# The chunk-wise inverse of the odd layer in 32x32 blocks, with two products per round side by side

## The reference, cut to what matters

```python
kk = jnp.einsum('bhntd,bhnsd->bhnts', kc, kc)
m = jnp.where(strict, betac[..., :, None] * kk * gam, 0.0)
rhs = jnp.concatenate([vc * betac[..., None], kc * (betac * jnp.exp(bc))[..., None]], axis=-1)
sol = lax.linalg.triangular_solve(m + jnp.eye(CHUNK, dtype=F32), rhs, left_side=True,
                                  lower=True, unit_diagonal=True)
u, w = sol[..., :C_DV], sol[..., C_DV:]
...
def step(state, xs):                      # over the 4 chunks
    v_new = u_i - w_i @ state
    o = qd_i @ state + qk_i @ v_new
    state = gl_i * state + kd_i.T @ v_new
```

## Time and profile before

| | us |
|---|---|
| median of 3 runs | 586.52 |
| profiled execution, device time | 586.91 |
| its span, first to last instruction | 584.7 |
| TensorE busy | 541.3 |
| VectorE busy | 328.9 |
| ScalarE busy | 254.0 |
| GpSimd busy | 81.4 |

### The profile page before, as it was taken

How to read it: one execution, slowest core, us unless ns; L and a number is a source line. 1 busy time by engine, 2 the same in 40 slices (tenths; PEclk the granted TensorE clock), 3 DMA queues, 4 the chain that set the end, 5 groups by cost and what they waited for, 6 DMA issues and landing times.

```text
span 584.7 us, 12159 instructions
## 1 busy us (share of the span) xinstructions
PE 541.3 (93%) x5162; PEld 445.5 (76%) x5162; DVE 328.9 (56%) x595; ACT 254.0 (43%) x501; POOL 81.4 (14%) x98
## 2 busy tenths in 40 slices
PE   6999799999899999789999999999999889999975
PEld 6999799996565645359989998999889656664632
DVE  3579876657334333377996555467445633334335
ACT  5576467664233323155546434433226323331311
POOL 5716621100000000021003900011110000000000
PEclk9999999998999999999999799999789989999999
DMA  9991333787899999997463430000315979989992
GB/s 319 272 371 58 108 109 110 228 305 295 312 408 409 375 411 409 390 376 243 160 215 80 176 109 2 4 4 2 145 34 225 411 282 411 408 347 412 407 409 109
DMA packets 55671, 144.16 MB, mean 247 GB/s; under 512 B 4292, under 2 KB 29088, under 8 KB 55488
## 3 DMA queue, kind: packets, MB, share of 16 engines
q1 hardware_dynamic: 54496, 141.88, 64.6%
q0 software_dynamic: 944, 1.41, 1.2%
q10 hardware_dynamic: 176, 0.07, 0.1%
HBM read 142.30 MB, written 1.05 MB: 245 GB/s over the span
## 4 chain that ended last, share of the span: by engine, by line
PE 75%; DVE 14%; ACT 5%; issue 3%; POOL 1%; DMA 1%; ACTq 0%; DVEq 0%
PE PS L2097 11%; PE PS L2058 7%; PE PS L2119 6%; PE PS L610 6%; PE PS L611 5%; PE PS L612 5%; PE PS L2133 4%; PE PS L646 3%; DVE WL L606 3%; PE PS L648 2%; PE PS L647 2%; PE PS L2134 2%; PE PS L2467 2%; PE PS L2488 2%; DVE SL L1303 2%
## 5 line engine op out<-in xcount | busy, mean ns | idle before, releaser
L606 DVE TENSOR_TENSOR WL<-RAW,WH 128x768 fp32r<-128x768 f32 (+2 forms) x90 | 82.0, 947 | 30.2 <-ACT WH L592 29.8
L610 PE MATMUL PS<-WH,HTH 128*128 128x384 f32 (+2 forms) x272 | 93.2, 343 | 3.0 <-DVE HTL L1295 1.4
L611 PE MATMUL PS<-WL,HTH 128*128 128x384 f32 (+2 forms) x272 | 90.1, 331 | 0.0
L612 PE MATMUL PS<-WH,HTL 128*128 128x384 f32 (+2 forms) x272 | 90.0, 331 | 0.0
L1295 DVE TENSOR_TENSOR X<-PS,X 128x512 f32<-128x512 f32 (+2 forms) x84 | 53.9, 663 | 48.0 <-PE PS L2134 36.1
L592 ACT ACTIVATE WH<-RAW 128x768 fp32r<-128x768 f32 (+2 forms) x90 | 67.2, 793 | 4.8 <-PE PS L612 3.1
L610 PEld LDWEIGHTS PS<-WH,HTH 128*128 128x128 f32 x272 | 53.5, 197 | 4.4 <-DVE HTL L1295 1.7
L611 PEld LDWEIGHTS PS<-WL,HTH 128*128 128x128 f32 x272 | 53.7, 197 | 0.0
L992 ACT ACTIVATE SIL<-PS,MW 128x128 f32<-128x128 f32 x18 | 6.6, 367 | 107.6 <-PE PS L2097 98.0
L612 PEld LDWEIGHTS PS<-WH,HTL 128*128 128x128 f32 x272 | 53.3, 196 | 0.0
L646 PE MATMUL PS<-HTH,WH 128*128 128x256 f32 x160 | 46.0, 287 | 0.4 <-DVE HTL L1303 0.4
(11 more groups left out here) (362 smaller groups left out, 1060.8 us busy)
## 6 DMA issues: line engine op xcount, KB each, us to landing
RAW<-moe_w_down SPq DMA_DIRECT2D x32, 512.0 KB, 13.1
RAW<-moe_w_gate SPq DMA_DIRECT2D x32, 512.0 KB, 7.8
RAW<-moe_w_up SPq DMA_DIRECT2D x32, 512.0 KB, 8.6
XD<-moe_w_down SPq DMA_DIRECT2D x32, 512.0 KB, 13.4
XG<-moe_w_gate SPq DMA_DIRECT2D x32, 512.0 KB, 9.2
XG<-moe_w_up SPq DMA_DIRECT2D x32, 512.0 KB, 10.3
RAW<-od_w_in SPq DMA_DIRECT2D x9, 1536.0 KB, 7.8
RAW<-ev_w_in SPq DMA_DIRECT2D x5, 1536.0 KB, 15.4
```

The costliest lines, as they stand in the source:

```text
L606: done(nc.vector.tensor_tensor(out=lo, in0=raw, in1=hi.bitcast(F32), op=ALU.subtract), "unit_lo")
L610: nc.tensor.matmul(ps, ah, bh, start=start, stop=False)
L611: nc.tensor.matmul(ps, ah, bl, start=False, stop=False)
L612: return nc.tensor.matmul(ps, al, bh, start=False, stop=stop)
```

## The change

The inverse inside a chunk is now built from 32x32 blocks for levels 0 to 4. The array is used as four 32x32 tiles on its diagonal (`quarters`), one per block of 32 frames. A round has two steps on TensorE instead of three. `inverse_TQ` issues the transpose of YC and the product of NTD with the half of YC's columns that this level uses (16 of 32 columns) into one bank; ScalarE copies both with one instruction of 384 columns (before: two of 512). `inverse_Z` multiplies the two (16 columns), and VectorE writes the result with two masked copies of 128 elements (before: one of 512). Level 0's entries come from a product with the identity (`inverse_N`) and the same masked copies, not from NTD directly. Level 5 joins 32x32 blocks in the same two steps with 64-wide pieces. Level 6 keeps 64x64 products, but its transpose is no longer waited for by its first product, and everything goes to `UT`, a full 128x128 block per head and tile whose zero quarter GpSimd clears. Each solve is then one 128x128 by 64 product per head instead of two. Group 1 stands one level behind group 0 in all engines' programs. The mask table grows by three 128-column layers, and on VectorE some elementwise steps of mixer D and of the gates stand later.

```diff
             def inverse_X(g, L):
-                rows = slice(0, P if L < 6 else CH)
                 act.wait_ge(sem(f"c_T{g}"), L)
-                done(nc.scalar.activation(heads(XC, g)[rows], level_ps(0, g)[rows], ACT.Copy), f"c_X{g}")
-
-            def inverse_Q(g, L):
-                rows = slice(0 if L < 6 else CH, P)
-                act.wait_ge(sem(f"c_Q{g}"), L)
-                done(nc.scalar.activation(heads(QC, g)[rows], level_ps(2, g)[rows], ACT.Copy), f"c_Qs{g}")
+                done(nc.scalar.activation(XC[:, g, :], PS[:, g, 0:384], ACT.Copy), f"c_X{g}")
+
+            def inverse_last_Q(g):
+                act.wait_ge(sem(f"c_Q{g}"), 1)
+                done(nc.scalar.activation(QC[CH:P, g, :, :], PS[CH:P, 2 + 2 * g, :].rearrange("p (n t) -> p n t", n=8), ACT.Copy),
+                     f"c_Qs{g}")
+            def inverse_upper(g, c):
+                act.wait_ge(sem(f"c_T{g}"), 6)
+                rows = slice(CH * c, CH * c + CH)
+                done(nc.scalar.activation(UT[rows, 0::2, 4 * g:4 * g + 4, rows],
+                                          PS[rows, g, :].rearrange("p (h i t) -> p i h t", h=4, i=2), ACT.Copy), f"c_Qs{g}")
...
+            inverse_X(0, 4)
+            inverse_X(1, 3)
+            inverse_X(0, 5)
+            inverse_X(1, 4)
+            inverse_last_Q(0)
+            inverse_upper(0, 1)
+            inverse_X(1, 5)
+            inverse_upper(0, 0)
+            inverse_last_Q(1)
+            inverse_upper(1, 1)
+            solved(0, 0, 1)
+            inverse_upper(1, 0)
+            solved(0, 1, 2)
-            solved(0, 0, 1)
-            solved(0, 1, 2)
...
+            def placed(g, L, b):
+
+                c = 2 ** (L + 1)
+                for half in range(2):
+                    cols = slice(32 * half, 32 * half + 32)
+                    to = YC[:, 4 * g:4 * g + 4, :, cols].rearrange("p h i (m c) -> p (h i) m c", c=c)[:, :, :, 0:c // 2]
+                    m1 = MKC[:, L, cols].rearrange("p (m c) -> p m c", c=c)[:, :, 0:c // 2]
+                    z = PS[:, b, 0:128].rearrange("p (n m c) -> p n m c", n=8, c=c // 2)
+                    done(nc.vector.copy_predicated(to, m1.unsqueeze(1).to_broadcast([P, 8, 32 // c, c // 2]), z), f"c_Y{g}")
...
+                if L < 5:
+                    placed(g, L, 2 + 2 * g)
...
                 else:
-                    done(nc.vector.tensor_copy(YS[0:CH, :, hs, :], z[0:CH]), f"c_Y{g}")
+                    z = PS[0:CH, 3 + 2 * g, :].rearrange("p (h i t) -> p i h t", h=4, i=2)
+                    done(nc.vector.tensor_copy(UT[0:CH, 0::2, hs, CH:P], z), "c_ys")
...
+            query_scores(2)
             dve.wait_ge(sem("dg_in"), 32)
             link(tt(xc2, xc2, bc(DG[:, :], 1, [P, 2, 512]), MUL))
-            inverse_level(0, 4)
-            inverse_level(1, 4)
-            query_scores(1)
+            inverse_level(1, 6)
+            query_scores(3)
             link(tt(xc2, xc2, bc(DB[:, :], 1, [P, 2, 512]), ADD))
+            residue(0, 1)
             dve.wait_ge(sem("gate_t"), 2)
             link(stt(tg, tg, 1.0, TM[:, :, 1552:2064], ADD, MUL))
-            inverse_level(0, 5)
-            inverse_level(1, 5)
             done(stt(TM[:, :, 1552:2064], xc2, 0.5, tg, MUL, MUL), "d_mix")
-            query_scores(2)
+            residue(1, 2)
+            out_split(1, 0)
+            lhs_lo(3, D_PIECES)
             dve.wait_ge(sem("gate_t"), 1)
             link(stt(SG[:, :, :], SG[:, :, :], 1.0, TM[:, :, 0:512], ADD, MUL))
-            inverse_level(0, 6)
-            inverse_level(1, 6)
-            query_scores(3)
             link(stt(g16, g16, 0.5, bc(CGAIN, 1, [P, 16, 64]), MUL, MUL))
-            out_split(1, 0)
-            lhs_lo(3, D_PIECES)
-            residue(0, 1)
             out_split(1, 1)
-            residue(1, 2)
             norm_sum(0, 0, 1)
             norm_sum(1, 0, 2)
...
-                return [(i, h) for i in range(NT) for h in range(4 * g, 4 * g + 4)]
+                return [(i, h) for h in range(4 * g, 4 * g + 4) for i in range(NT)]
...
+            def inverse_N(g):
+                pe.wait_ge(sem("c_nt"), 2 * g + 1)
+                for n, (i, h) in enumerate(group(g)):
+                    for q, rows in enumerate(quarters):
+                        last = mm(PS[rows, g, 16 * n:16 * n + 16], key_block(q, i, h), first_half(ident[rows, rows], 0),
+                                  start=True, stop=True)
+                done(last, f"c_N{g}")
...
+            def inverse_TQ(g, L):
+                pe.wait_ge(sem(f"c_Y{g}"), 2 * L)
+                if L < 5:
+                    for n, (i, h) in enumerate(group(g)):
+                        for q, rows in enumerate(quarters):
+                            mm(PS[rows, g, 32 * n:32 * n + 32], inverse_block(q, i, h), ident[rows, rows], start=True, stop=True)
+                    for n, (i, h) in enumerate(group(g)):
+                        o = 256 + 16 * n
+                        for q, rows in enumerate(quarters):
+                            last = mm(PS[rows, g, o:o + 16], key_block(q, i, h), first_half(inverse_block(q, i, h), L),
+                                      start=True, stop=True)
...
+                    for i, h in group(g):
+                        o = CH * (h % 4)
+                        for c, rows in enumerate(halves):
+                            mm(PS[strip(c, i), g, o:o + CH], YC[rows, h, i, 32:64], ident[rows, rows], start=True, stop=True)
+                    for i, h in group(g):
+                        o = 256 + 32 * (h % 4)
+                        for c, rows in enumerate(halves):
+                            b = 256 * i + CH * c + 32
+                            last = mm(PS[strip(c, i), g, o:o + 32], NTD[rows, h, b:b + 32], YC[rows, h, i, 0:32], start=True, stop=True)
                 done(last, f"c_T{g}")
...
+                for n, (i, h) in enumerate(group(g)):
+                    if L < 5:
+                        for q, rows in enumerate(quarters):
+                            last = mm(PS[rows, 2 + 2 * g, 16 * n:16 * n + 16], XC[rows, g, 32 * n:32 * n + 32],
+                                      XC[rows, g, 256 + 16 * n:256 + 16 * n + 16], start=True, stop=True)
...
+            def inverse_last(g):
+                pe.wait_ge(sem(f"c_Y{g}"), 12)
+                for n, (i, h) in enumerate(group(g)):
+                    last = mm(PS[high, 2 + 2 * g, CH * n:CH * n + CH], NTD[low, h, 256 * i + CH:256 * i + P], YC[low, h, i, :],
+                              start=True, stop=True)
                 done(last, f"c_Q{g}")
+                for n, (i, h) in enumerate(group(g)):
+                    for rows in halves:
+                        last = mm(PS[rows, g, CH * n:CH * n + CH], YC[rows, h, i, :], ident[rows, rows], start=True, stop=True)
+                done(last, f"c_T{g}")
+
+            def inverse_last_Z(g):
+                pe.wait_ge(sem(f"c_Qs{g}"), 2)
+                for n, (i, h) in enumerate(group(g)):
+                    last = mm(PS[low, 3 + 2 * g, CH * n:CH * n + CH], QC[high, g, n, :], UT[high, 2 * i, h, CH:P], start=True, stop=True)
                 done(last, f"c_Z{g}")
...
                 for h in range(4 * g, 4 * g + 4):
                     hs = slice(256 * i + (h % 4) * 64, 256 * i + (h % 4) * 64 + 64)
-                    mm(PS[low, 2 * i + g, hs], YC[low, i, h, :], rhs[low, h, :], start=True, stop=True)
-                    last = mm(PS[high, 2 * i + g, hs], YS[:, i, h, :], rhs[:, h, :], start=True, stop=True)
+                    last = mm(PS[:, 2 * i + g, hs], UT[:, 2 * i, h, :], rhs[:, h, :], start=True, stop=True)
                 done(last, "c_U")
...
             pe.wait_ge(sem("proj_ev"), proj_total[1])
+            inverse_N(0)
             key_scores(1)
+            inverse_TQ(0, 1)
             retention_scores(1)
-            pe.wait_ge(sem("c_nt"), 3)
-            for L in range(1, 7):
-                inverse_T(0, L)
-                inverse_T(1, L)
+            pe.wait_ge(sem("c_nt"), 2)
+            inverse_Z(0, 1)
+            inverse_N(1)
+            inverse_TQ(0, 2)
+            inverse_TQ(1, 1)
+            retention_out()
+            inverse_Z(0, 2)
+            inverse_Z(1, 1)
+            inverse_TQ(0, 3)
+            inverse_TQ(1, 2)
+            inverse_Z(0, 3)
+            inverse_Z(1, 2)
+            values_T()
+            inverse_TQ(0, 4)
+            inverse_TQ(1, 3)
+            inverse_Z(0, 4)
+            inverse_Z(1, 3)
+            query_scores(0)
+            inverse_TQ(0, 5)
+            inverse_TQ(1, 4)
+            inverse_Z(0, 5)
+            inverse_Z(1, 4)
+            query_scores(1)
+            inverse_last(0)
+            inverse_TQ(1, 5)
+            inverse_last_Z(0)
+            inverse_Z(1, 5)
+            query_scores(2)
+            inverse_last(1)
             first_rows(0)
+            query_scores(3)
+            inverse_last_Z(1)
+            residue(0, 1)
             first_rows(1)
```

(62 more changed lines are left out.)

96 lines of the change are left out of this document (39 added, 57 removed).

## The result

| | before | changed |
|---|---|---|
| median of runs (5 of each), us | 586.25 | 604.99 |
| lowest to highest, us | 584.36 to 588.19 | 601.68 to 612.72 |
| profiled span, us | 584.7 | 603.2 |
| first record of the output projection, us | 420.31 | 440.27 |
| from there to the end of the span, us | 164.4 | 162.9 |

The ratio is 1.0321, with a 95% interval of 1.0275 to 1.0367. The forecast was 576.1, range 571 to 588: wrong in its sign, and outside its range. The last two lines of the table say where to look: all of the loss lies ahead of the first output unit, where I had forecast 9 us of gain.

The account below looks back on a forecast made before the run. TensorE's pace was taken as the bound. 15.9 us of its work removed, less 5.5 of added waits, gave 10.4 off the profiled 586.9, so 576.5, and a median of 576.1; range 571 to 588.

Parts of the forecast that it names:

- TensorE's pace: Inverse levels: four 32x32 blocks side by side take 8.3 ns a record, so 1,664 records take 13.8 us.
- My own sign for it: In a T step, 64 records would start over 0.5 us, not 0.9 or more.
- The burst of 10 ns: Layer 0 before the change: four records in different blocks start within 0.03 us, at most 10 ns apart.
- the 20 ns over 48 records: Layer 0 before the change: fastest sustained pace seen, four positions used, a third of the records with 128 columns moving.
- Rival A: TensorE cannot issue faster than seen sustained: 594.5 at 20 ns a record, 611.4 at 29.2; chance 0.12 and 0.03.
- Waits laid bare: TensorE's idle in the inverse and its tail grows from 2.7 to 8.2 us, 5.5 more.
- The three waits of the tail: After `inverse_last_Z(1)`, TensorE waits 0.8 us for the residue, 0.75 for `d_mix` and 3.0 before `outputs(1, 0)`.
- Masked copies: VectorE's 128-element copies in the inverse levels take 0.35 us each, two 0.7, as much as the one before.
- The solves: Four solves after the inverse go from 8.2 us to 3.4, at 8 records per call and 104 ns each.
- The clock: One fall to half clock expected again in the new tail, as before, costing 3.3 us: no gain and no loss.
- Rival B: Half clock in the 32-wide stretch, levels 1 to 4: some 15 us more, 591; chance 0.05.
- a sign of being wrong: Records over 12 ns apart, VectorE taking over the chain, or the clock at 0.5 before the solves.

Follow-up runs that it names:

- the streams: Kernel before with two streams of unused independent products, 32x32 then 64x64, 2,048 records each, put ahead of the first solve; the streams took 56 and 58 us.

## Why the prediction was wrong

**The step that failed is TensorE's pace.** I took 8.3 ns a record "because rows 3 and 4 show the block's own time and not the issue deciding", over 1,664 records. The block's time was right (8.6 ns measured). My own sign for it, 64 records of a T step starting over 0.5 us, came true (0.55) while the kernel lost. A record also needs two instructions, and I never asked whether these can be had at that rate; the term has no line for them. The burst of 10 ns in the earlier trace rows is shorter than a piece of 256 instructions, so it could not show this; the 20 ns over 48 records are no limit either, for the same reason. The price that counts is 27.5 to 28.5 ns a record when it goes on (29.1 over the twelve pieces of the changed kernel), and the steps of the kernel before, at 29.2 ns, stood only 2 to 6% above the streams' price. The query scores between them give some room: with them a round is 200 records in 6.61 us, 33 ns each.

**The sum with the right term.** 1,664 records are 3,328 instructions, 13 pieces, and at 3.5 us each 46 us. I had 13.8 for their array time, 32 less. The first output unit was forecast about 9 us before 420.31, near 411, and came at 440.27, 29 later. So this one term accounts for the miss in its size.

**Rival A was the right one**, with 0.15 of the chance. Its first price (20 ns, 594.5) was too low, its second (29.2 ns, 611.4) 6 us too high. It added the price of the small records to that of the wide products beside them, but pieces keep coming under those: from 376.77 to 387.96 three pieces came, 3.73 us each, though 24 of their records are retention products that alone hold TensorE for 5.2 us. The argument against it was the burst. The Trainium skill ("TensorE: Matmul & The Clock Gate", "Wait — 56ns, not 53.3ns?") led to an estimate near 604 by another reason, a start-to-start floor near 25 ns. The time fits, the reason does not: within a piece records started 8.6 ns apart. The Trainium skill ("Runtime: NRT & Kernel Launch", "Instruction fetch mechanics") states that instructions come in blocks of 16 KiB, 256 of them, each fetched while the one before runs, and that this is mostly hidden. The trace agrees on the size (14 packets of 16 KB, stops 128 records or a multiple of them apart) and not on the hiding, once records are cheaper than about 28 ns.

**Waits laid bare.** The three waits of the tail were forecast as 0.8, 0.75 and 3.0, and were 0.44, 0.39 and 2.24: right in place, somewhat large. Those in the levels could not show. Masked copies were forecast at 0.35 and took 0.28 to 0.48.

**The solves** were forecast to gain 4.8 us and gained 8.6 alone: my sum of TensorE work was right (4.5), and the rest came behind it, with a higher clock.

**The clock** was forecast with one fall. Rival B, the half clock in the 32-wide stretch, had 0.05, and its condition came: 0.56 in 371.0 to 399.7, and 0.5 before the solves, which I had named as a sign of being wrong. It fell five times (369.7, 386.8, 403.9, 414.1 and 438.0), each in or right behind a stop or a wait. In 355 to 443 its mean is 0.74 for 0.94. It is no cause of the pieces' pace: the streams took nearly the same time a piece at either level. A burst of 128 records lasts longer at half clock, and the stop behind it is shorter: in the 32x32 stream 1.28 + 2.45 us at full clock (from 408.51) and 1.93 + 1.80 at half (from 437.52), 3.73 both times. So the half clock adds to TensorE's busy time there and not to the kernel's. What the falls cost behind the last stop, at 414.1 and 438.0, was not taken apart.

## What to carry to other kernels

Count instructions and not only array time: for any stretch of small TensorE products, take (loads + matmuls) / 256 times 3.5 us as a floor beside the sum of durations, and look at the packets of the instruction queue for how near it is already. Here blocks cut smaller than 64x64 cost more, however little they computed; fewer and larger instructions that do needless work (a full 128x128 transpose, a 128x128 solve) won. A pace read from a burst shorter than 256 instructions says nothing of what can be kept up. And where a chain ends in a tail of dependent products, an independent unit put ahead of the last wait paid twice here, by the wait and by the clock that did not fall.

## What the runs showed of the hardware

- TensorE's instruction supply: 256 instructions per 3.45 to 4.0 us, 27.5 ns a record for 32x32 and 28.5 for 64x64, at 0.55 and at 0.97 of the clock, with no other traffic; 3.73 us a piece over the twelve of the changed kernel. TensorE then stalls, mostly for 1.1 to 2.5 us at a time and in the middle of a step; the trace calls it issue.
- Array time of a 32x32 record in four places: 8.6 ns at full clock; 128 at half clock start over some 1.7 us, 13 ns each. A 64x64 record in four places at full clock: 1.87 us for 128, some 15 ns.
- Idle time of 3 us in TensorE's tail was followed by a stretch at 0.60 of the clock; without the idle time it stayed at 1.00 under the same products.
